# A decoder trunk in one kernel: the second layer's output projection begun inside the new tokens' attention batches

## The reference

```python
def combine_groups(outs, lses):
    wts = jax.nn.softmax(jnp.stack(lses, axis=0), axis=0)
    return jnp.einsum('gnts,gntsd->ntsd', wts.astype(outs[0].dtype), jnp.stack(outs, axis=0))
...
            op = dilated_prompt(qp, kbp, vbp, slopes_b)
            osm = dilated_sample(qs, kcb, vcb, slopes_b)
            xp = xp + op.reshape(bp, tp, B_SLOTS * HEAD_DIM) @ w_o_b[b]
            xs = xs + osm.reshape(bs, ts, B_SLOTS * HEAD_DIM) @ w_o_b[b]
        xp = xp + swiglu(rms_norm(xp, g_ffn[l]), w_gate_up[l], w_down[l])
        xs = xs + swiglu(rms_norm(xs, g_ffn[l]), w_gate_up[l], w_down[l])
```

## Time and profile before

| | us |
|---|---|
| median of 3 runs | 2608.94 |
| lowest and highest | 2607.05 and 2609.13 |
| the profiled execution, by the clock of the runs | 2609.32 |
| span of the profiled execution | 2607.5 |
| PE busy | 2507.1 (96%) |
| DVE, ACT, POOL busy | 1004.1, 663.5, 432.9 |

### The profile page before, as it was taken

How to read it: one execution, slowest core, us unless ns; L and a number is a source line. 1 busy time by engine, 2 the same in 40 slices (tenths; PEclk the granted TensorE clock), 3 DMA queues, 4 the chain that set the end, 5 groups by cost and what they waited for, 6 DMA issues and landing times. The chain is left out here.

```text
span 2607.5 us, 42354 instructions
## 1 busy us (share of the span) xinstructions
PE 2507.1 (96%) x16451; PEld 2426.9 (93%) x16451; DVE 1004.1 (39%) x1989; ACT 663.5 (25%) x1265; POOL 432.9 (17%) x456
## 2 busy tenths in 40 slices
PE   7989899999999999999999999789999999999997
PEld 7878699999999999999999899469999999999997
DVE  6465635322332232336212466436332232232335
ACT  4344423211111111123100367224320111111113
POOL 2343201101100101101111433431100100100100
PEclk9999999999999999999999999899999999999999
DMA  4010214113111312101211233843111211311312
GB/s 170 20 51 17 86 42 134 48 36 110 47 36 53 105 36 102 63 31 51 91 59 40 90 95 109 302 167 112 48 33 56 104 41 42 111 39 50 112 33 84
DMA packets 67236, 199.26 MB, mean 76 GB/s; under 512 B 7704, under 2 KB 14232, under 8 KB 66360
## 3 DMA queue, kind: packets, MB, share of 16 engines
q1 hardware_dynamic: 66232, 193.17, 22.0%
q0 software_dynamic: 912, 4.85, 0.5%
HBM read 182.21 MB, written 51.05 MB: 89 GB/s over the span
## 5 line engine op out<-in xcount | busy, mean ns | idle before, releaser
L936 DVE TENSOR_TENSOR WL<-RAW,WH 128x1024 fp32r<-128x1024 f32 (+3 forms) x198 | 219.8, 1111 | 1166.2 <-ACT WH L616 1165.5
L1467 PE MATMUL PS<-XH,WH 128*128 128x384 f32 x2832 | 624.0, 330 | 11.4 <-DVE XL L963 8.1
L1467 PE MATMUL PS<-XH,WL 128*128 128x384 f32 (+1 forms) x2736 | 605.5, 329 | 0.0
L1467 PE MATMUL PS<-XL,WH 128*128 128x384 f32 x2640 | 583.8, 329 | 0.0
L1467 PEld LDWEIGHTS PS<-XH,WH 128*128 128x128 f32 x2832 | 486.8, 189 | 13.1 <-issue 12.0
L466 POOL TENSOR_TENSOR RAW<-RAW,GAIN 128x1024 f32<-128x1024 f32 x114 | 221.8, 1947 | 1657.4 <-DMA RAW<-in_w_gu 1394.8
L616 ACT CAST WH<-RAW 128x1024 fp32r<-128x1024 f32 (+3 forms) x198 | 186.9, 945 | 1185.4 <-PE PS L1467 1160.2
L1467 PEld LDWEIGHTS PS<-XH,WL 128*128 128x128 f32 x2736 | 469.9, 189 | 0.0
L1467 PEld LDWEIGHTS PS<-XL,WH 128*128 128x128 f32 x2640 | 452.7, 188 | 0.0
L1467 PE MATMUL PS<-HH,WH 128*128 128x384 f32 (+1 forms) x1041 | 228.6, 327 | 0.0
L1467 PE MATMUL PS<-HH,WL 128*128 128x384 f32 (+1 forms) x1041 | 228.5, 327 | 0.0
(11 more groups left out here) (215 smaller groups left out, 2569.0 us busy)
## 6 DMA issues: line engine op xcount, KB each, us to landing
RAW<-in_w_gu SPq DMA_DIRECT2D x88, 512.0 KB, 3.5
out_bkS<-in_bk_in SPq DMA_DIRECT2D x8, 2032.0 KB
out_bvS<-in_bv_in SPq DMA_DIRECT2D x8, 2032.0 KB
RAW<-in_w_dn SPq DMA_DIRECT2D x32, 384.0 KB, 2.9
KC<-in_bk_in SPq DMA_DIRECT2D x8, 1536.0 KB, 9.4
VC<-in_bv_in SPq DMA_DIRECT2D x8, 1536.0 KB, 6.9
RAW<-in_w_dn SPq DMA_DIRECT2D x32, 320.0 KB, 2.8
XT<-in_xT SPq DMA_DIRECT2D x16, 544.0 KB, 4.6
```

The source lines that it names most:

```text
L936: nc.vector.tensor_tensor(lo[:, j, 0:nk * P], RAW[:, j, 0:nk * P], hi[:, j, 0:nk * P].bitcast(F32), ALU.subtract).then_inc(S["wl"], 1)
L1467: ins = mm(PS[:, 3 * j + c, 0:width], w[:, j, k * P:(k + 1) * P], x(k, a, width), start=(k == 0 and n == 0), stop=(k == nk - 1 and n == 2))
```

## The change

- **Merges ahead.** `MERGES` gives the tile merged in each batch: 0; 1 and 2; 3; 4 and 5; 6 and 7; all are turned by batch 5. OM and the coefficients have two buffers. On POOL the queries of batch i+2 stand before the merges of batch i.
- **Units.** A unit is 12 matmuls, one chunk of 384 tokens of one oB output tile. The 16 units of chunks 0 and 1 are placed by `UNITS` between the parts of batches 3 to 7, three in each and four in the last. DVE adds each to the residual (`add_unit`, L1423). Chunk 2 (320 tokens, those of the new sequences among them) follows as `rest`, 8 times 12 matmuls (L1926, added at L1431).
- **Weights of oB** are loaded and split once into OBH and OBL, which stay for all 8 tiles: two tiles at the end of each of batches 0 to 3. SP issues the loads between KC and VC.
- **PSUM and buffers.** The turned-back output moves from bank 2 to bank 7; units use bank 2, odd ones from 9 on bank 0. The squares of this norm use a buffer of their own, SQB.
- **Behind.** gu10's first weights are loaded when `rest(0)` is done; their low parts stand on DVE before the last two `add_rest`; all XL tiles stand behind the last addition and the squares of tile 6.
- All loops over batches are written out.

The diff, cut:

```diff
+        MERGES = {0: (0,), 1: (1, 2), 2: (3,), 3: (4, 5), 4: (6, 7)}
+        UNITS = {3: (0, 1, 2), 4: (3, 4, 5), 5: (6, 7, 8), 6: (9, 10, 11), 7: (12, 13, 14, 15)}
...
+            out_weights(0)
+            sp.wait_ge(S["sb_s"], 1)
+            sp.dma_start(KC[:, 0], keys_of(2)).then_inc(S["kc0"], 16)
+            for i in range(NEWB):
+                for m in MERGES.get(i - 1, ()):
+                    if m < 6:
+                        sp.wait_ge(S["m_om"], m + 1)
+                        merge_load(m + 2)
+                b = i + 3
+                if b < NEWB:
                     sp.wait_ge(S["sb_s"], b - 1)
-                    sp.dma_start(KC[:, j], keys_of(b)).then_inc(S[f"kc{j}"], 16)
+                    sp.dma_start(KC[:, b % 2], keys_of(b)).then_inc(S[f"kc{b % 2}"], 16)
+                if 0 < i < 4:
+                    out_weights(i)
...
-            slabs("oB", t["w_oB"])
+            sp.wait_ge(S["slab"], PLAN.first["oB"] + 1)
...
+            sample(0, 0)
+            sample(1, 0)
+            for i in range(NEWB):
+                if i + 2 < NEWB:
+                    sample(i + 2, 1 + max(MERGES.get(i - 1, (-1 if i == 0 else 7,))))
+                for m in MERGES.get(i, ()):
+                    merge(m, min(i + 3, NEWB))
...
-                if not (isinstance(b, int) and b == 0):
-                    dve.wait_ge(S["m_om"], b)
+                if m >= 2:
+                    dve.wait_ge(S["m_om"], m - 1)
...
+            for i in range(NEWB):
+                if i + 1 < NEWB:
+                    sample(i + 1)
+                sample_keys(i)
+                for m in MERGES.get(i, ()):
+                    weights(m)
+                if i + 1 < NEWB:
+                    sums(i + 1)
+                turned, units = MERGES.get(i - 1, ()), UNITS.get(i, ())
+                for q in units[:1]:
+                    add_unit(q)
+                for m in turned[:1]:
+                    merge_out(m)
+                for q in units[1:2]:
+                    add_unit(q)
+                sample_out(i)
+                for m in turned[1:]:
+                    merge_out(m)
+                for q in units[2:]:
+                    add_unit(q)
+                if i < 4:
+                    split_out(2 * i)
+                    split_out(2 * i + 1)
             dve.wait_ge(S["rows_out"], 80)
-            t_phase("oB", evac_res(3, late=True), peel=True)
-            after_o(3, "oB")
+            for o in range(KT):
+                if o >= KT - 2:
+                    split_lo(PLAN.first["gu10"] + o % 2, o % 2, KT)
+                add_rest(o)
+                if o:
+                    add_squares(3, o - 1, (o - 1) % 2)
+            dve.wait_ge(S["slab"], PLAN.end("oB"))
+            for k in range(KT):
+                low(3, k)
+            add_squares(3, KT - 1, 1)
...
+            def unit(q):
+                c, o = q // 8, q % 8
+                a, width = CH[c]
+                pe.wait_ge(S["wl"], PLAN.first["oB"] + o + 1)
+                pe.wait_ge(S["m_lo"], 8 if bank_u(q) == 0 else 3 * c + 3)
+                if q:
+                    pe.wait_ge(S["ob_evac"], q if q < 9 else q - 1)
+                for k in range(4):
+                    for n, (w, z) in enumerate(((OBH, 0), (OBH, 4), (OBL, 0))):
+                        ins = mm(PS[:, bank_u(q), 0:width], w[o][:, k * P:(k + 1) * P], XH[:, (z + k) * TOK + a:(z + k) * TOK + a + width],
+                                 start=(k == 0 and n == 0), stop=(k == 3 and n == 2))
...
+            for i in range(NEWB):
+                if i + 1 < NEWB:
+                    sample_scores(i + 1, (i + 1) % 2)
+                turned, units = MERGES.get(i - 1, ()), UNITS.get(i, ())
+                sample_turn(i)
+                for q in units[:1]:
+                    unit(q)
+                sample_values(i)
+                for m in turned[:1]:
+                    merged(m)
+                for q in units[1:2]:
+                    unit(q)
+                sample_back(i)
+                for m in turned[1:]:
+                    merged(m)
+                for q in units[2:]:
+                    unit(q)
             pe.wait_ge(S["sb_ol"], 16)
-            pe.wait_ge(S["m_lo"], 8)
-            t_phase("oB", tiles(XH), tiles(XH, 4), None)
+            for o in range(KT):
+                rest(o)
```

More of the change, by code:

```diff
@@ L129, in program @@
         EPSB = at("EPSB", [P, 1], take(4))
-        SM = at("SM", [P, 96], take(384))
+        SM = at("SM", [P, 128], take(512))
         R = base[0]
@@ L890, in _, with split_out @@
-            batch(0, 0)
-            batch(1, 1)
-            def pair(i):
-                batch(2 * i, 0)
-                batch(2 * i + 1, 1)
-            loop(act, 1, 4, pair)
-            batch(8, 0)
-            merge_out(7)
-            act.wait_ge(S["rows_out"], 80)
-            start("oB")
-            t_phase("oB", evac_sq(3, "oB"))
+            def split_out(o):
+                s = PLAN.first["oB"] + o
+                act.wait_ge(S[f"raw{o % 2}"], 16 * raw_count(s, o % 2))
+                nc.scalar.copy(OBH[o][:], RAW[:, o % 2, 0:512]).then_inc(S["wh"], 1)
@@ L903, in _ @@
+            for i in range(4):
+                for j in range(2):
+                    if i == 3:
+                        split_hi("gu10", j, j, WH, 6 - j)
+                    evac_sq(3, "oB")(i, j, PLAN.first["oB"] + 2 * i + j)
             after_o(3, "oB")
@@ L1357, in sample_keys @@
             def sample_keys(b):
                 dve.wait_ge(S["sb_tr"], 2 * b + 2)
-                if not (isinstance(b, int) and b == 0):
+                if b:
                     dve.wait_ge(S["sb_pv"], b)
@@ new lines, in add_unit, with add_rest @@
+            def add_unit(q):
+                a, w = CH[q // 8]
+                dve.wait_ge(S["ob_unit"], q + 1)
+                x = XT[:, (q % 8) * TOK + a:(q % 8) * TOK + a + w]
+                nc.vector.tensor_tensor(x, x, PS[:, bank_u(q), 0:w], ALU.add).then_inc(S["ob_evac"], 1)
+            def add_rest(o):
+                j = o % 2
+                a, w = CH[2]
+                dve.wait_ge(S["slab"], PLAN.first["oB"] + o + 1)
+                x = XT[:, o * TOK + a:o * TOK + a + w]
+                nc.vector.tensor_tensor(x, x, PS[:, 3 * j + 2, 0:w], ALU.add).then_inc(S[f"free{j}"], 1)
@@ L1827, in sample_scores, with merged, rest, sample_turn @@
                 ins.then_inc(S["sb_s"], 1)
[L1829 to L1833 removed]
+            def merged(m):
+                pe.wait_ge(S["m_om"], m + 1)
+                if m:
+                    pe.wait_ge(S["m_lo"], m)
                 for c in range(4):
[L1835 removed]
+                    ins = nc.tensor.transpose(PS[:, 0, c * P:(c + 1) * P], OM[:, m % 2, c * P:(c + 1) * P], IDN[:])
                 ins.then_inc(S["m_tr"], 1)
[L1838 removed]
+            def unit(q):
[9 more added lines that the diff above has]
+                                 start=(k == 0 and n == 0), stop=(k == 3 and n == 2))
+                ins.then_inc(S["ob_unit"], 1)
+            def rest(o):
+                a, width = CH[2]
+                j = o % 2
+                if o == 0:
+                    pe.wait_ge(S["ob_evac"], 16)
+                else:
+                    pe.wait_ge(S[f"free{j}"], PLAN.groups["oB"] + o // 2)
+                for k in range(4):
+                    for n, (w, z) in enumerate(((OBH, 0), (OBH, 4), (OBL, 0))):
+                        ins = mm(PS[:, 3 * j + 2, 0:width], w[o][:, k * P:(k + 1) * P], XH[:, (z + k) * TOK + a:(z + k) * TOK + a + width],
+                                 start=(k == 0 and n == 0), stop=(k == 3 and n == 2))
+                ins.then_inc(S["slab"], 1)
+            def sample_turn(b):
+                j = b % 2
                 pe.wait_ge(S["sb_exp"], b + 1)
```

253 lines of the change are left out of this document (114 added, 139 removed).

## The result

| | before | after |
|---|---|---|
| median of 20 runs, us | 2607.9 | 2611.4 |
| span of the profiled execution, us | 2607.5 | 2610.1 |
| first scores to gu10's first matmul, us | 162.5 | 163.8 |
| from there to the last matmul, us | 803.0 | 804.2 |

The ratio of the runs is 1.0016, with a 95% interval of 1.0009 to 1.0022. One of the 20 executions of the kernel before took 4161.9 us, far from all others; without it the median is 2607.8. The forecast was 2608 us, a gain of 1.3; the time went the other way by 3.6. The interval leaves no room for a gain, though the loss is under the 0.2% that the forecast counted as a change.

The account below looks back on a forecast made before the run. Batches were bound by a PE-POOL cycle over OM, not PE. 1680.3 + 40.1 + 33.3 + 12.5 + 3 = 1769.2 for `rest`, plus 24.5 puts gu10 at 1793.7 against 1795.0: about 2608 us, range 2596 to 2619.

Parts of the forecast that it names:

- (6): Outside the edited stretch: nothing moves, so the median shifts only by gu10's earlier start, 2608.9 - 1.3, about 2608 us.
- (1): Batches 0 to 2: no change, scores 4 start at 1680.3 as now; bounds 1672 and 1684.
- (2): PE's work in batches 3 to 7: 40.1 us, plus 16 units at 2.08 each, 33.3 us.
- (3): PE's waits in batches 3 to 7, from POOL's merges holding DVE: 5.6 (unit 1), 4.3 (unit 4), 2.6 (batch 3's values), together 12.5.
- (4): PE's clock in batches 3 to 7: three waits cost 1 us each in lowered clock, 3 us.
- (5): From the start of `rest` to gu10: 24.5 us against 55.1 now, including 3.8 of POOL's scalings holding up DVE.
- A: Rival: DVE and POOL do not meet, (3) falls to about 1; 2594 us, chance 0.14, its half (2601) 0.18.
- B: Rival: units among waits fall to 1.2 GHz, 4.2 us instead of 2.08; 8 net, 2616 us, slower; chance 0.14.
- C: Rival: DMA loads of weights and merges delay values and keys, stretching batches 1 and 2; +6, 2614 to 2615; chance 0.12.

Follow-up runs that it names:

- e1: The kernel before with only the small tile SM widened from 96 to 128 columns, so tiles behind it lie 128 bytes higher; ratio 1.0016 to the kernel before.

## Why the prediction was wrong, and where it held

- **The step that failed is (6)**, "elsewhere nothing moves". The instructions outside the stretch are the same, but their addresses are not: SM's 128 bytes slowed some 3100 matmuls by 1.1 ns, 3.4 us. e1 shows it alone at 1.0016. Put into the forecast in place of nothing, this term alone turns its gain of 1.3 into a loss of 2.1. No rival named it; the widened tile stood in the change.
- **(1) held**: scores 4 began 48.3 us after the first ones (47.8 forecast and before).
- **(2) was mis-sized.** A unit took 2.17 us or more among other work, not 2.08, which is the price inside a longer run: 1.9 us over 16 units. From the first start of a unit to its third it took 0.42 to 0.46 us where other work stood ahead, as in unit 9, and 0.35 in unit 15, which follows unit 14:

```profile
1748.47 0.62 PE L1912 MATMUL PS<-XH,OBH 128*128 128x384 f32 x2
1748.93 0.34 PE L1912 MATMUL PS<-XH,OBL 128*128 128x384 f32 x1
...
1768.64 0.51 PE L1912 MATMUL PS<-XH,OBH 128*128 128x384 f32 x2
1768.99 0.33 PE L1912 MATMUL PS<-XH,OBL 128*128 128x384 f32 x1
```

- **(3) held in sum**, 12.1 us of waits against 12.5, but not in its parts, and the near sum is luck: 3.85 and 2.86 for units 1 and 4 instead of 5.6 and 4.3, 3.91 instead of 2.6 for the values of batch 3, and 1.5 in three small ones (0.53, 0.19, 0.74) that the forecast did not have. The values hung on weights that landed late, not on splits caught by a merge:

```profile
1686.90 1.30 ACT L908 CAST OBH<-RAW 128x512 fp32r<-128x512 f32 x2 [5.19 <-DMA RAW<-in_w_oB]
```

- **(4) held**: unit 1 took 3.99 and unit 4 3.10 instead of 2.2, and the transposes ahead of unit 1 1.11 instead of 0.66, with 0.61 of the clock granted from 1694 to 1707, 3.2 us against 3:

```profile
1694.00:1707.00 13.00, 8.63 (x56) 7.12 (x48) 6.79 (x17) 2.46 (x7) 11.18 (x10) 0.61 0.75 266
```

- **(5) held**: 24.85 against 24.5. Three sums of squares met POOL's scalings and took 2.43, 2.58 and 2.67 instead of 1.28, 3.8 in all. The forecast had the same 3.8 from two scalings; the third sum met that of a third slab, which it had not counted.
- **Rivals.** A lost: the engines met as forecast. B lost: of 16 units two ran below full clock, and the first matmuls of unit 5. C lost: the batches ahead did not stretch, and transfers held PE up only through the output weights. The net of the stretch is +1.2 where -1.3 was forecast, most of it from the size of a unit. Kernels with the same schedule there differ by up to 1.7, so this part of the miss is not certain, as that of (6) is.

## What to carry to other kernels

A tile that grows moves all tiles behind it. Where the moving operand and the weights of a dense matmul phase changed their distance, the pace changed by 0.7% here, and a padding of 128 bytes gave 8.6 us, where the schedule as first built gave nothing. Work put into idle time of the bound engine needs its consumer's place in the other engine's order looked at first: an addition that stands behind unrelated work hands that work's every delay to PE. Waits in series hide each other, so edits that gained 0.7, 3.4 and 8.4 us alone gave 18.8 together here.

## What the runs showed of the hardware

The start-to-start time of fp32r matmuls in a dense phase depended on the distance between the addresses of the moving operand and the weights: 165.55 ns on average where it was an odd multiple of 128 bytes (18304 or 78464), 166.67 where it was a multiple of 256 (18432 or 78336), over chunks of 384, 384 and 320 columns, in fourteen kernels with five layouts. DVE's instructions with two SBUF inputs took turns with POOL's tensor operations: a coefficient instruction of 0.17 to 0.18 us lasted up to 1.00, to the end of the POOL instruction that ran. A DVE addition with one input in PSUM kept its 0.53 us.
